# Key and query norms of a gated delta rule, taken from the key products and put into the output norm, in an eight-stage kernel on one core

## What is computed

```
def _l2norm(xf):
    return xf * lax.rsqrt(jnp.sum(xf * xf, axis=-1, keepdims=True) + EPS)

q = _l2norm(q.reshape(bsz, s, h, d)) * (d ** -0.5)
k = _l2norm(k.reshape(bsz, s, h, d))
beta = jax.nn.sigmoid(b)
g = -jnp.exp(a_log) * jax.nn.softplus(a + dt_bias)
decay = exp(gcum_i - gcum_j), i >= j          # gcum: running sum of g
m = where(i > j, (k_i * beta_i) . k_j * decay, 0)
t_mat = inverse of (1 + m)
u_base = t_mat @ (v * beta)
w_mat = t_mat @ (k * beta * exp(gcum))
qk = q . k * decay
# chunk by chunk: u = u_base - w_mat @ state;  o = q_dec @ state + qk @ u;  state = ...
o = _rms_f32(o) * norm_w * jax.nn.silu(gate)
```

## Time and profile before

| | |
|---|---|
| median of three runs | 1105.55 us |
| the profiled execution, device time | 1104.8 us |
| its span, first to last instruction | 1102.9 us |
| mean granted TensorE clock | 0.999 |
| TensorE busy (matmuls) | 1089.6 us, 99% |
| TensorE weight loads | 879.0 us, 80% |
| VectorE busy | 668.8 us, 61% |
| ScalarE busy | 465.4 us, 42% |
| GpSimd busy | 502.6 us, 46% |
| DMA | 97.28 MB, mean 88 GB/s |

### The profile page before, as it was taken

How to read it: one execution, slowest core, us unless ns; L and a number is a source line. 1 busy time by engine, 2 the same in 40 slices (tenths; PEclk the granted TensorE clock), 3 DMA queues, 4 the chain that set the end, 5 groups by cost and what they waited for, 6 DMA issues and landing times.

```text
span 1102.9 us, 16220 instructions
## 1 busy us (share of the span) xinstructions
PE 1089.6 (99%) x5922; PEld 879.0 (80%) x5922; DVE 668.8 (61%) x958; ACT 465.4 (42%) x808; POOL 502.6 (46%) x375
## 2 busy tenths in 40 slices
PE   9999999999999999999999999999999999999997
PEld 7786877788788888888888888877778778888786
DVE  6875986416666666666641222548754757986863
ACT  6436321354744333333333334345464543243663
POOL 5445341122455444444444445433347686632441
PEclk9999999999999999999999999999999999999999
DMA  9953532241223323232323325322115222212222
GB/s 246 136 85 56 67 70 39 84 108 39 78 90 102 114 76 114 76 114 76 114 74 98 105 78 152 115 77 77 39 52 140 54 80 78 77 40 78 77 77 77
DMA packets 101721, 97.28 MB, mean 88 GB/s; under 512 B 4896, under 2 KB 95776, under 8 KB 101280
## 3 DMA queue, kind: packets, MB, share of 16 engines
q1 hardware_dynamic: 101232, 95.71, 31.8%
q10 hardware_dynamic: 432, 0.79, 0.2%
HBM read 94.38 MB, written 2.10 MB: 87 GB/s over the span
## 4 chain that ended last, share of the span: by engine, by line
PE 91%; DVE 4%; ACT 2%; issue 1%; POOL 1%; DMA 1%; POOLq 0%; DVEq 0%; SPq 0%; ACTq 0%
PE ps L1914 26%; PE ps L1916 25%; PE ps L1915 25%; PE ps L2457 4%; PE ps L2118 1%; DVE x_a L1237 1%; DVE conv L1758 1%; PE ps L2392 1%; ACT x_a L674 1%; PE ps L2403 1%; PE ps L2304 1%; PE ps L2286 1%; DVE tt L1349 1%; POOL w_lo L536 1%; PE ps L2380 1%
## 5 line engine op out<-in xcount | busy, mean ns | idle before, releaser
L536 POOL TENSOR_TENSOR w_lo<-raw,w_hi 128x512 fp32r<-128x512 f32 (+1 forms) x330 | 447.9, 1368 | 568.1 <-ACT w_hi L657 557.5
L657 ACT ACTIVATE w_hi<-raw 128x512 fp32r<-128x512 f32 (+1 forms) x330 | 201.1, 620 | 254.1 <-PE ps L1916 237.2
L1914 PE MATMUL ps<-x_a,w_hi 128*128 128x512 f32 x624 | 251.8, 403 | 4.3 <-POOL w_lo L536 2.0
L1916 PE MATMUL ps<-x_a,w_lo 128*128 128x512 f32 x624 | 243.3, 390 | 0.0
L1915 PE MATMUL ps<-x_a,w_hi 128*128 128x512 f32 x624 | 243.3, 390 | 0.0
L1914 PE MATMUL ps<-x_b,w_hi 128*128 128x512 f32 x416 | 162.5, 391 | 0.1
L1915 PE MATMUL ps<-x_b,w_hi 128*128 128x512 f32 x416 | 161.9, 389 | 0.0
L1916 PE MATMUL ps<-x_b,w_lo 128*128 128x512 f32 x416 | 161.8, 389 | 0.0
L1914 PEld LDWEIGHTS ps<-x_a,w_hi 128*128 128x128 f32 x624 | 117.2, 188 | 38.9 <-issue 11.1
L1916 PEld LDWEIGHTS ps<-x_a,w_lo 128*128 128x128 f32 x624 | 117.1, 188 | 24.9
L1915 PEld LDWEIGHTS ps<-x_a,w_hi 128*128 128x128 f32 x624 | 117.3, 188 | 24.6 <-issue 2.2
(11 more groups left out here) (351 smaller groups left out, 1532.2 us busy)
## 6 DMA issues: line engine op xcount, KB each, us to landing
raw<-in_w_up SPq DMA_DIRECT2D x44, 512.0 KB, 4.4
raw<-in_w_in SPq DMA_DIRECT2D x31, 512.0 KB, 7.7
raw<-in_c_w_in SPq DMA_DIRECT2D x24, 512.0 KB, 4.7
raw<-in_a_w_in SPq DMA_DIRECT2D x18, 512.0 KB, 4.6
raw<-in_w_down SPq DMA_DIRECT2D x16, 512.0 KB, 4.4
raw<-in_w_out SPq DMA_DIRECT2D x8, 512.0 KB, 4.0
raw<-in_c_w_out SPq DMA_DIRECT2D x8, 512.0 KB, 4.1
raw<-in_w_down SPq DMA_DIRECT2D x8, 384.0 KB, 3.4
```

The lines of the kernel that those rows point to most:

```text
L536: nc.gpsimd.tensor_tensor(ring_half(WL, n), raw_half(n), f32(ring_half(WH, n)), SUB) \
L657: nc.scalar.activation(ring_half(WH, n), raw_half(n), ACT.Copy).then_inc(w_hi, 1)
L1914: mm(out, w_hi_, x_hi_, start=first, stop=False)
L1916: return mm(out, w_lo_, x_hi_, start=False, stop=last)
```

## The change

The keys and queries stay as they come out of SiLU. The key products move from behind unit 15 to behind unit 12 and are made of the raw keys; ScalarE copies them to SBUF (GRAM). Their diagonal holds the squares of the key norms: VectorE masks it with the identity (DIAG) and reduces it to 16 columns (KSSQ), ScalarE makes 1/norm of these (RKN). The norms then go into the small per-token factors: VBETA = beta/norm for the values, KBETA = beta/norm squared for LB and for BEN. `gb_ready` is now signalled by KBETA. M is made from GRAM in SBUF. The query products move from behind unit 16 to behind unit 15. Both sums of squares with ones, both large scalings and their Ln and Exp are gone. The query norm scales all outputs of a token alike, so it is left out and only the constant under the output norm's root changes: the raw queries' squares, times P² EPS, are added to the outputs' squares (QSQ), with a new bias of P EPS². For that ScalarE squares the raw queries at unit 25, the squares of the first three output chunks are taken ahead of the last one, and VectorE adds the two in two pieces.

```diff
@@ -166,9 +166,10 @@
...
         QKT = at("qkt", [P, NB * H, P], F32, AR + 57344)
-        R4 = at("r4", [P, H, S], F32, AR + 57344)
+        GRAM = at("k_gram", [P, NB * H, P], F32, AR + 57344)
+        DIAG = at("k_gram_diagonal", [P, NB * H, P], F32, AR + 65536)
+        QSQ = at("q_sq_and_o_sq", [P, H, S], F32, AR + 112640)
         EB = at("eb", [P, NB * H, P], F32, AR + 65536)
-        SQ4 = at("sq4", [P, H, S], F32, AR + 65536)
@@ -204,6 +205,10 @@
...
         BETA = SM[:, 3, :]
+        RKN = SM[:, 0, :]
+        VBETA = SM[:, 1, :]
+        KBETA = SM[:, 9, :]
+        KSSQ = SM[:, 10, :]
@@ -542,7 +547,7 @@
...
             nc.gpsimd.memset(CB[:, 0:1], EPS).then_inc(ones_ready, 1)
-            nc.gpsimd.memset(CB[:, 1:2], math.log(P ** -0.5)).then_inc(ones_ready, 1)
+            nc.gpsimd.memset(CB[:, 1:2], EPS * EPS * P).then_inc(ones_ready, 1)
@@ -555,7 +560,7 @@
...
             nc.gpsimd.tensor_tensor(LB[:, :, :], LOWER.unsqueeze(1).broadcast_to([P, 16, P]),
-                                    BETA.unsqueeze(2).broadcast_to([P, 16, P]), MUL).then_inc(lb_ready, 1)
+                                    KBETA.unsqueeze(2).broadcast_to([P, 16, P]), MUL).then_inc(lb_ready, 1)
@@ -746,7 +751,7 @@
...
                     nc.scalar.activation(VB[:, h, :], PS[:, 5, h * P:(h + 1) * P], ACT.Copy,
-                                         scale=BETA[:, 4 * c + h:4 * c + h + 1]).then_inc(tokv_ready, 1)
+                                         scale=VBETA[:, 4 * c + h:4 * c + h + 1]).then_inc(tokv_ready, 1)
@@ -773,6 +778,13 @@
...
+            def output_squares(c, n):
...
+                act.wait_ge(op_src, 4)
+                act.wait_ge(o_ready, c + n)
+                nc.scalar.activation(RR[:, :, c * P:(c + n) * P], KQ[:, :, 1, c * P:(c + n) * P], ACT.Square) \
+                    .then_inc(rsq_ready, 1)
@@ -800,9 +812,6 @@
...
                     tile_silu(i)
-                if u == 6:
-                    act.wait_ge(silu_done, 4)
-                    nc.scalar.activation(SQ4[:, :, :], KQ[:, :, 0, :], ACT.Square).then_inc(sqk, 1)
@@ -813,17 +822,13 @@
...
-                    act.wait_ge(ssq_filled, 1)
-                    step(nc.scalar.activation(R4[:, :, :], MX, ACT.Ln, bias=CB[:, 0:1]))
-                    nc.scalar.activation(R4[:, :, :], R4[:, :, :], ACT.Exp, scale=-0.5).then_inc(r4_ready, 1)
-                    nc.scalar.activation(SQ4[:, :, :], KQ[:, :, 1, :], ACT.Square).then_inc(sqk, 1)
+                    act.wait_ge(g_filled, 1)
+                    nc.scalar.activation(GRAM[:, :, :].rearrange("p a i -> p (a i)"),
+                                         MX.rearrange("p b s -> p (b s)"), ACT.Copy).then_inc(g_copied, 1)
...
-                    act.wait_ge(ssq_filled, 2)
-                    act.wait_ge(kq_normed, 1)
-                    step(nc.scalar.activation(R4[:, :, :], MX, ACT.Ln, bias=CB[:, 0:1]))
-                    nc.scalar.activation(R4[:, :, :], R4[:, :, :], ACT.Exp, scale=-0.5, bias=CB[:, 1:2]) \
-                        .then_inc(r4_ready, 1)
+                    act.wait_ge(kssq_ready, 1)
+                    step(nc.scalar.activation(RKN, KSSQ, ACT.Ln, bias=CB[:, 0:1]))
+                    nc.scalar.activation(RKN, RKN, ACT.Exp, scale=-0.5).then_inc(rk_ready, 1)
@@ -859,6 +864,10 @@
...
                     ret_norm(0)
+                    act.wait_ge(ro_filled, 4)
+                    act.wait_ge(qk_filled, 1)
+                    nc.scalar.activation(QSQ[:, :, :], KQ[:, :, 1, :], ACT.Square, scale=P * EPS ** 0.5) \
+                        .then_inc(rsq_ready, 1)
@@ -880,6 +889,8 @@
...
+                    output_squares(0, 3)
@@ -887,10 +898,7 @@
...
                     outputs(3)
-                    act.wait_ge(o_ready, 4)
-                    act.wait_ge(op_src, 4)
-                    for h in range(H):
-                        nc.scalar.activation(RR[:, h, :], KQ[:, h, 1, :], ACT.Square).then_inc(rsq_ready, 1)
+                    output_squares(3, 1)
@@ -900,7 +908,7 @@
...
                 act.wait_ge(rssq_filled, 2 + h + 1)
-                step(nc.scalar.activation(RR[:, h, :], MX[:, h, :], ACT.Ln, bias=CB[:, 0:1], scale=1.0 / P))
+                step(nc.scalar.activation(RR[:, h, :], MX[:, h, :], ACT.Ln, bias=CB[:, 1:2], scale=1.0 / P))
@@ -1408,6 +1416,12 @@
...
+            def add_output_squares(c, n):
...
+                dve.wait_ge(rsq_ready, 3 if c == 0 else 4)
+                q = QSQ[:, :, c * P:(c + n) * P]
+                v.tensor_tensor(q, q, RR[:, :, c * P:(c + n) * P], ADD).then_inc(osq_added, 1)
@@ -1433,21 +1447,24 @@
...
                     step(v.tensor_scalar(SPB, SPB, 1.0, None, ADD))
-                    v.reciprocal(BETA, SPB).then_inc(gb_ready, 1)
+                    step(v.reciprocal(BETA, SPB))
...
                         .then_inc(gu_ready, 1)
-                    dve.wait_ge(r4_ready, 1)
-                    v.tensor_tensor(KQ[:, :, 0, :], KQ[:, :, 0, :], R4[:, :, :], MUL).then_inc(kq_normed, 1)
+                    dve.wait_ge(g_copied, 1)
+                    step(v.tensor_tensor(DIAG[:, :, :], GRAM[:, :, :],
+                                         IDENT[:, :].unsqueeze(1).broadcast_to([P, 16, P]), MUL))
+                    v.tensor_reduce(KSSQ, DIAG[:, :, :], AX.X, ADD).then_inc(kssq_ready, 1)
...
                     step(v.tensor_tensor(CS[:, 1, :], CS[:, 1, :], RSTD[:, :], MUL))
-                    dve.wait_ge(r4_ready, 2)
-                    v.tensor_tensor(KQ[:, :, 1, :], KQ[:, :, 1, :], R4[:, :, :], MUL).then_inc(kq_normed, 1)
+                    dve.wait_ge(rk_ready, 1)
+                    step(v.tensor_tensor(VBETA, BETA, RKN, MUL))
+                    v.tensor_tensor(KBETA, VBETA, RKN, MUL).then_inc(gb_ready, 1)
...
                     dve.wait_ge(eb_ready, 1)
-                    step(v.scalar_tensor_tensor(out=BEN, in0=BETA, scalar=-1.0, in1=EGC, op0=MUL, op1=MUL))
+                    step(v.scalar_tensor_tensor(out=BEN, in0=KBETA, scalar=-1.0, in1=EGC, op0=MUL, op1=MUL))
@@ -1477,6 +1494,7 @@
...
                 if u == 31:
+                    add_output_squares(0, 3)
@@ -1497,8 +1515,7 @@
...
                     step(v.tensor_tensor(M[:, :, :], M[:, :, :], LB[:, :, :], MUL))
-                    dve.wait_ge(g_filled, 1)
-                    v.tensor_tensor(M[:, :, :], MX16, M[:, :, :], MUL).then_inc(m_ready, 1)
+                    v.tensor_tensor(M[:, :, :], GRAM[:, :, :], M[:, :, :], MUL).then_inc(m_ready, 1)
@@ -1522,9 +1539,9 @@
...
+            add_output_squares(3, 1)
...
             for h in range(H):
-                dve.wait_ge(rsq_ready, 1 + h + 1)
@@ -1935,9 +1952,9 @@
...
                 pe.wait_ge(o_ready, 4)
+                pe.wait_ge(osq_added, 2)
                 for h in range(H):
-                    pe.wait_ge(rsq_ready, 1 + h + 1)
-                    mm(PS[:, 4 + h, :], ONES[:, :], RR[:, h, :], start=True, stop=True).then_inc(rssq_filled, 1)
+                    mm(PS[:, 4 + h, :], ONES[:, :], QSQ[:, h, :], start=True, stop=True).then_inc(rssq_filled, 1)
@@ -2270,40 +2287,37 @@
...
                     ins.then_inc(abt_filled, 1)
-                if u == 12 or u == 13:
+                if u == 12:
...
                     pe.wait_ge(conv_ready, 12)
-                    pe.wait_ge(sqk, u - 11)
-                    pe.wait_ge(sp_in, 1)
+                    pe.wait_ge(silu_done, 4)
                     pe.wait_ge(rcol_ready, 1)
-                    if u == 13:
-                        pe.wait_ge(r4_ready, 1)
-                        pe.wait_ge(gu_ready, 1)
-                        mm(PS[:, 4, 0:16], UPPER, GG, start=True, stop=True).then_inc(gc_filled, 1)
-                    for h in (1, 2, 3, 0):
-                        if h == 0 and u == 13:
-                            pe.wait_ge(gc_ready, 1)
-                        ins = mm(PS[:, 4 + h, :], ONES[:, :], SQ4[:, h, :], start=True, stop=True)
-                    ins.then_inc(ssq_filled, 1)
+                    for c in range(NB):
+                        for h in range(H):
+                            ins = mm(PS[:, 4 + c, h * P:(h + 1) * P], KQ[:, h, 0, c * P:(c + 1) * P],
+                                     KQ[:, h, 0, c * P:(c + 1) * P], start=True, stop=True)
+                    ins.then_inc(g_filled, 1)
+                if u == 13:
+                    pe.wait_ge(g_copied, 1)
+                    pe.wait_ge(gu_ready, 1)
+                    mm(PS[:, 4, 0:16], UPPER, GG, start=True, stop=True).then_inc(gc_filled, 1)
...
-                    pe.wait_ge(r4_ready, 2)
+                    pe.wait_ge(gc_ready, 1)
...
                     ins.then_inc(gcb_filled, 1)
-                if u == 15 or u == 16:
...
-                    if u == 15:
-                        pe.wait_ge(x1_ready, 1)
-                        pe.wait_ge(kq_normed, 2)
-                    else:
-                        pe.wait_ge(m_ready, 1)
+                if u == 15:
...
+                    pe.wait_ge(x1_ready, 1)
```

(10 more changed lines are left out.)

## The result

The changed kernel took 1111.71 us (median of 5 runs, 1110.71 to 1112.3), the kernel before 1105.15 us (median of 5 runs, 1104.78 to 1106.0). The ratio is 1.0058, with a 95% interval of 1.0047 to 1.0069: slower by 0.6%. The forecast was 1113.2 us, with a range of 1108.5 to 1117.0.

The account below looks back on a forecast made before the run. TensorE was taken to bound the kernel. Matmuls -6.9, wait +9.1, clock +2.3, given back +3.6, output norm -0.4 made +7.7 us: 1104.8 to 1112.5 profiled, with 0.75 for the median 1113.2, range 1108.5 to 1117.0.

Parts of the forecast that it names:

- The matmuls: TensorE around units 12 to 17: sums of squares gone and products moved, 3.3 us less before unit 14, 6.9 in all.
- The wait at unit 14: TensorE waits 9.1 us at unit 14 for GpSimd's low half, which is made only behind the later LB.
- The chain: Unit 12's end to gb_ready: products, copy, mask, reduction, norms and factors put gb_ready at 97.8, 9.6 us later.
- my lower bound: GpSimd's LB ahead of unit 14: at least 5.2 us, four times the 1.29 of a 512-column split.
- The clock: Behind the wait at unit 14: idleness lowers TensorE's clock, costing 2.3 us as at the kernel's start.
- no fall: Rival behind unit 14's wait: TensorE resumes at full clock, +5.4 us, 1110.9; chance 0.18.
- The given-back part: Units 17, 20 and 21 move with m_ready, so 3.6 us of saved matmul time return as short waits.
- only the first wait: Rival behind unit 14: VectorE's chain runs faster and TensorE doesn't wait for it, +4.1 us, 1109.6; chance 0.08.
- The output norm: Near unit 32: fewer squares behind the last output chunk, so the matmul at 293.19 wins about 0.4 us.
- TensorE never waits: Rival at unit 14: halves done by 95.5, so the matmul saving comes off whole, -7.3 us, 1098.2; chance 0.07.
- the step before it in the same text: Slow chain behind unit 14: unit 21 needs the bank VectorE's shuffle frees, with no slack, and begins 8.1 us later.

Follow-up runs that it names:

- version with the splits first: The changed kernel with GpSimd making the low weight halves of units 14 and 15 ahead of LB instead of behind it; 1100.32 us.
- 30 spare matmuls: The changed kernel with 30 unused float32 matmuls of 128 columns on TensorE behind the product GC, inside the wait at unit 14; 1109.76 us.
- three changes of VectorE's list: Version with the splits first, plus GRAM times LB formed ahead of EB, rotations of tiles 16 and 17 behind block inversion, tile 19's behind the inverse's first level; 1097.49 us.
- version with both edits: Version with the splits first, without GpSimd's wait for M ahead of unit 17's splits and with tile 17 rotated ahead of three 2048-column products; 1102.55 us.
- version with the rotations behind: Version with the splits first, with GRAM times LB formed ahead of EB and rotations of tiles 16 and 17 behind the block inversion; 1100.72 us.

## Why the prediction came out as it did

It was right in sign and nearly in size: +6.7 us in the profiled execution, forecast +7.7, and each term was found in its place. All of them up to the seam of unit 32 come from starts that can be read in both traces.

*The matmuls: -7.5 us, forecast -6.9.* The version with the splits first has the same matmuls and no wait at unit 14. There it is 9.5 us from unit 12's end to unit 14's second matmul (85.92 to 95.41), in the kernel before 13.4 (85.61 to 99.03). That is 3.9 us less, where I had 3.3, and 3.57 behind unit 16 as forecast. The mis-sized term is GC: I had 0.8 us for it with the gap ahead of it, and it takes 0.23 without one: from its start (94.95) to unit 14's second matmul it is 0.46, of which 0.23 are unit 14's first.

*The wait at unit 14: +7.9 us, forecast +9.1.* From GC to unit 14's second matmul it is 8.58 us (94.51 to 103.09), without the wait 0.46 (94.95 to 95.41); 0.2 of the difference is the clock's. The profile puts the wait at 7.72. The chain was sized well: mask 2.29, reduction 2.29 at 1.04 ns a column as I had carried it over from the rows of 512 and 1024 columns, copy 1.89, `gb_ready` at 97.5 against 97.8. The mis-sized term is LB: 3.61 us, not 5.53, nor even my lower bound of 5.2. Before, LB ran beside a 2048-column product of VectorE; here nothing of VectorE's runs beside it, which I had used for VectorE's small products (0.68 us, forecast 0.69) and not for GpSimd's. The kernel before with LB held back to 105.88 shows that it is this and not the new factor: there LB takes 3.61 us too, and VectorE is idle beside it. The bound failed because I took four splits for it: alone, a split costs 2.5 ns a column (1.29 us for 512) and this product 1.76 (3.61 for 2048).

*The clock: +2.4 us, forecast +2.3.* Twelve matmuls of 0.43 instead of 0.227 us. The 30 spare matmuls gave back 2.0. That the start's 2.3 us would also be the price here was a guess from one row, and it came out. The rival "no fall" (1110.9) is nearer the median than the forecast is, but only because LB was sized too long: its mechanism is excluded by the granted clock of 0.50.

The Trainium skill, TensorE: Matmul & The Clock Gate, Part 1, gives 426.7 ns from start to start for 512 columns at the lower of the two clocks and 215.7 at the upper. The trace agrees with the first (0.43) and has 0.227 for the second in this kernel. By the rule that idleness brings the lower one back, as I had weighed it, the fall was to come, and it did.

*The given-back part: +3.5 us up to unit 21, forecast +3.6.* It is what is left of unit 21's shift (6.17 us, 147.52 to 153.69) behind the three terms above, with unit 12's end 0.1 us earlier. The profile shows 2.6 of it as waits, of 1.1, 0.6, 0.3 and 0.6 us at units 17, 20 and 21; where the rest lies isn't shown. M's signal moved by 6.3 us (121.97 to 128.26), the shuffle's end from 147.41 to 153.64, 6.2 us: the old distances held, as I had said, and so the rival "only the first wait" fell. Another 0.4 us came at retention's state (`ret_s`, 0.9 us in three waits, before 0.5), which no step had.

*The output norm: -0.8 us, forecast -0.4.* The first residual of unit 32 begins 5.8 us later than before, the sums' operand 6.6 us later. The wait that ended at 293.19 is gone.

*Sum:* -7.5 + 7.9 + 2.4 + 3.5 + 0.4 - 0.8 = +5.9 us, less the 0.1 by which unit 12 ended earlier, is 5.8, and this shift holds to the start of VectorE's last operation (1105.1 against 1099.4). The remaining 0.9 of this execution's 6.7 lie behind it, mostly in the last output's transfer (4.5 us from there to the end of the span, before 3.5). I don't know its cause; the medians of five differ by 6.6. Without these 0.9 us the forecast would have been 1.9 us too high for this execution, the size of LB's error; that it came within 1 us is in part luck.

*The rival that was priced wrong* is "TensorE never waits", at -7.3 us. When its condition was made true (the splits first), the kernel took 1100.3 us, so -4.8. It went by the saving alone, though the step before it in the same text said that VectorE's chain had no slack at unit 21. The 3.6 us that I counted as given back because of the wait are given back without it too (3.5): a saving in TensorE's work behind unit 14 can't pass a bank that VectorE frees no sooner. With them the rival's price is 1101.8 instead of 1098.2, 1.5 above what was measured. It took three changes of VectorE's list together to let the saving pass; with one and with two of them the times were 1102.25 and 1100.72 us. Which of the three are needed, and whether the rotation of tile 19 alone would have done on the version with the splits first, wasn't tried.

## What to carry to other kernels

Where each engine runs a list of its own in order, price an edit by what stands *behind* each wait that it moves: a weight split that has nothing to do with the new value stood behind it, and 7.5 us of saved matmuls became a loss of 6.6 until it was moved ahead. Before counting a saving on the bounding engine, look for the next place where another engine releases it with no slack, for the saving ends there. Then move that engine's work into its idle time ahead of the release, or behind it, and look at the waits again after each step: here the first two steps moved the wait to a place where it cost as much, and only the third got through. Several short waits were better here than one of nearly their sum, since they left the clock up.

## What the runs showed of the hardware that was not expected

- The clock falls after waits much shorter than the one that I had priced: at 2.56 us (0.66 in the window), at 2.4 us (0.88 then 0.78), at 2.1 us (0.78, loads at 0.33 from 142.97 to 145.96), and at 1.54 us among small matmuls (0.85 then 0.50; in another version 0.69 then 0.63). It is not the length alone: a wait of 1.6 us at unit 20, among matmuls of 512 columns, left it at 1.00 (the version with both edits), as did waits of 1.1, 0.4, 0.3 and 0.5 us, one after the other. Nor is it the same in every execution: the version with the rotations behind took 1099.29 us at a mean clock of 1.0 and 1101.97 at 0.996. The extra cost in the kernel before was 1.5 us behind 2.56 us of waiting and 2.5 behind 11.54.
- What runs beside it sets the price of an instruction on GpSimd: LB took 5.53 us beside a VectorE product of 2048 columns, 4.08 beside one of 512 (which itself took 4.10, not 0.69), 3.61 alone. It holds the other way round too: in the version with the splits first, a 16-column operation of VectorE that began just behind LB took 3.61 us, as long as LB, where one of its kind takes 0.18.
- A float32 matmul of 128 columns, of the plain kind, costs 0.22 us at full clock with its two records.
